# Pooled projection computed channel-major, its running sums by doubling on VectorE and GpSimd in place of banded products on TensorE, and three waits moved

## What is computed

```python
def multiscale_pool(xp):                      # windows 2, 4, 8, 16 for four groups of 256 channels
    cs = pad(cumsum(xp, axis=1))
    lo = maximum(t + 1 - w, 0); cnt = minimum(t + 1, w)
    means[g] = (cs[t + 1] - cs[lo]) / cnt     # mean over the last w tokens
    return concatenate(means) - xp
mix = multiscale_pool(xp)
yb = einsum('bsgc,gcd->bsgd', mix, pool_w) * pool_scale * silu(zp)
```

## Time and profile before

| | |
|---|---|
| median of three runs | 789.54 us |
| the profiled execution's own time | 788.85 us |
| its span (first to last instruction) | 787.0 us |
| PE busy | 775.4 us, 99% |
| DVE busy | 558.2 us, 71% |
| ACT busy | 440.7 us, 56% |
| POOL busy | 131.9 us, 17% |
| granted PE clock | full speed in every slice but the start |

### The profile page before, as it was taken

The page is one execution under the profiler, slowest core; times in us unless marked ns, Lnnn a source line. Parts: engine busy times, 40 slices in busy tenths (PEclk is TensorE's granted clock), DMA queues, the critical chain, the costliest instruction groups (busy, mean ns, idle before and its releaser), DMA issues.

```text
span 787.0 us, 11898 instructions
## 1 busy us (share of the span) xinstructions
PE 775.4 (99%) x4592; PEld 682.2 (87%) x4592; DVE 558.2 (71%) x899; ACT 440.7 (56%) x613; POOL 131.9 (17%) x103
## 2 busy tenths in 40 slices
PE   9999999999999999999999999999999999999998
PEld 7777778888888899999988888999799878978886
DVE  5655565885468687787873476688875896898785
ACT  6755674345443575565644374555856344889650
POOL 0002930000000004444441000014005000006000
PEclk9999999999999999999999999999999999999999
DMA  9987434344454565554545446435465416544211
GB/s 339 406 292 250 177 137 157 134 138 157 170 203 161 199 235 199 183 193 167 207 162 202 177 148 222 151 118 201 161 239 189 156 59 214 202 173 161 107 55 54
DMA packets 23364, 142.78 MB, mean 181 GB/s; under 512 B 3564, under 2 KB 4472, under 8 KB 7312
## 3 DMA queue, kind: packets, MB, share of 16 engines
q1 hardware_dynamic: 20160, 134.51, 47.7%
q10 hardware_dynamic: 1776, 4.12, 1.4%
q0 software_dynamic: 1376, 3.43, 1.2%
HBM read 140.97 MB, written 2.64 MB: 182 GB/s over the span
## 4 chain that ended last, share of the span: by engine, by line
PE 83%; DVE 8%; DMA 3%; ACT 3%; issue 2%; SPq 0%; ACTq 0%; DVEq 0%
PE gemm L496 16%; PE gemm L498 16%; PE gemm L497 16%; PE gemm L502 8%; PE gemm L504 8%; PE gemm L503 8%; DMA raw<-in_weights 2%; DVE wlo L1744 2%; DVE xc L2290 2%; ACT whi L1201 2%; PE head L560 1%; DMA xres<-in_x 1%; PE head L779 1%; PE head L935 1%; PE head L913 1%
## 5 line engine op out<-in xcount | busy, mean ns | idle before, releaser
L1744 DVE TENSOR_TENSOR wlo<-raw,whi 128x2048 fp32r<-128x2048 f32 x119 | 275.6, 2317 | 102.7 <-ACT whi L1201 102.6
L1201 ACT CAST whi<-raw 128x2048 fp32r<-128x2048 f32 x120 | 228.8, 1907 | 193.3 <-PE gemm L498 114.9
L496 PE MATMUL gemm<-whi,x0hi 128*128 128x512 f32 (+2 forms) x400 | 157.7, 394 | 1.0 <-DVE wlo L1744 1.0
L498 PE MATMUL gemm<-whi,x0lo 128*128 128x512 f32 (+2 forms) x400 | 154.0, 385 | 0.0
L497 PE MATMUL gemm<-wlo,x0hi 128*128 128x512 f32 (+2 forms) x400 | 153.6, 384 | 0.0
L502 PE MATMUL gemm<-x1hi,whi 128*128 128x256 f32 x400 | 113.6, 284 | 0.0
L504 PE MATMUL gemm<-x1hi,wlo 128*128 128x256 f32 x400 | 113.2, 283 | 0.0
L503 PE MATMUL gemm<-x1lo,whi 128*128 128x256 f32 x400 | 113.2, 283 | 0.0
L496 PEld LDWEIGHTS gemm<-whi,x0hi 128*128 128x128 f32 x400 | 75.1, 188 | 17.5 <-DVE wlo L1744 2.3
L498 PEld LDWEIGHTS gemm<-whi,x0lo 128*128 128x128 f32 x400 | 75.1, 188 | 15.0
L497 PEld LDWEIGHTS gemm<-wlo,x0hi 128*128 128x128 f32 x400 | 75.2, 188 | 13.4
(11 more groups left out here) (367 smaller groups left out, 1328.3 us busy)
## 6 DMA issues: line engine op xcount, KB each, us to landing
raw<-in_weights SPq DMA_DIRECT2D x122, 1024.0 KB, 4.8
raw<-in_weights SPq DMA_DIRECT2D x4, 512.0 KB, 6.2
bias_rows<-bias_row POOLq DMA_DIRECT2D x1, 1536.0 KB, 19.6
memt<-in_memt SPq DMA_DIRECT2D x4, 256.0 KB, 5.2
tok<-in_mem SPq DMA_DIRECT2D x1, 1024.0 KB, 7.1
xt<-in_xt SPq DMA_DIRECT2D x2, 512.0 KB, 10.9
xres<-in_x ACTq DMA_DIRECT2D x1, 1024.0 KB, 9.1
bias<-bias_rows POOLq DMA_DIRECT2D x8, 128.0 KB, 5.2
```

The costliest lines, as they stand in the source:

```text
L496: mm(o, xh, wh, start=start, stop=False)
L498: return mm(o, xl, wh, start=False, stop=stop)
L1201: nc.scalar.copy(whi[:, p % RING, :], raw[:, p % RING, :]).then_inc(s_hi, 1)
L1744: V.tensor_tensor(wlo[:, p % RING, :], raw[:, p % RING, :], whi[:, p % RING, :].bitcast(F32), ALU.subtract).then_inc(s_lo, 1)
```

## The change

- `xp` becomes channel-major (`crossed_channels`), 48 matmuls a piece. DVE scales it by `rrow` while it empties it into `xpc`, which has 8 zero columns ahead of each channel's 256 tokens. `row_copy(2)` moves from step 78 to the end of step 77 on ACT.
- `pool_mix` goes. Sums over 2, 4, 8 and 16 tokens are made by doubling: a tile plus itself shifted by 1, 2, 4, 8 columns. DVE does groups 0 and 1 at step 78 and group 2 at step 79, POOL group 3. DVE then corrects the first 16 tokens, divides and subtracts `xp` in place (`window_mean`), for all four groups.
- `x1hi` and `x1lo` are made from `xpc` in SBUF, not from PSUM, one step earlier (79 to 82).
- ACT splits piece 85 early in step 83; DVE does so after it has emptied the `pool` chunks, no longer before.
- At step 82 DVE empties `zp` and makes `x1lo` before the gate rows.
- `dm` has its own place, so POOL no longer waits for `s_mixm` ahead of its DMAs; the 1 MB constant `poolb` becomes the small `icnt`.
- The three waits: squares of `mix` at step 4; the first `down` (and `aout`) piece does its two column halves in turn and waits for each half's bank alone; the split of piece 123 comes ahead of the last `olo`.

```diff
-    ("xp", 4, 2, "act"), ...
+    ("xp", 4, 2, "dve"), ...
-SCALED = {"mem": 0, "mix": 3, ...
+SCALED = {"mem": 0, "mix": 4, ...
-LATE_SPLIT = (p0("pool"), p0("up"), ...
+LATE_SPLIT = (p0("up"), ...
...
+            def crossed_channels(p, name, i_):
+                c = c0(name) + i_ % 2
+                if i_ < 2:
+                    chunk_free(pe, c - 2)
+                r = p % RING
+                for b in range(4):
+                    for j in range(4):
+                        kb = 4 * (i_ // 2) + j
+                        ws = slice(j * 512 + b * P, j * 512 + b * P + P)
+                        i = passes_t(bank(c, b // 2)[:, b % 2 * S:b % 2 * S + S], x0hi[:, kb, :], x0lo[:, kb, :],
+                                     whi[:, r, ws], wlo[:, r, ws], kb == 0 and b % 2 == 0, kb == KB - 1 and b % 2 == 1)
+                return i
...
-            def pool_mix(p):
...
                 elif name in ("down", "aout"):
-                    if i_ == 0:
-                        chunk_free(pe, c - 2)
-                        chunk_free(pe, c - 1)
-                    for t in range(T):
-                        for h in range(2):
+                    for h in range(2):
+                        if i_ == 0:
+                            chunk_free(pe, c - 2 + h)
+                        for t in range(T):
                             i = k_major(p, name, i_, h, t, src, i_ == 0, False)
...
+                if p == p0("xp") + 2:
+                    row_copy(2)
+                if p0("zp") <= p < p0("pool"):
+                    b = p - p0("zp")
                     act.wait_ge(s_mixm, b + 1)
+                    nc.scalar.copy(x1hi[:, 2 * b:2 * b + 2, :], xpc[:, 2 * b:2 * b + 2, PAD:PAD + S]).then_inc(s_mixhi, 1)
...
+            def window_sums(g):
+                chunk_free(dve, c0("xp") + g // 2)
+                if g:
+                    dve.wait_ge(s_mixm, g)
+                x = xpc[:, 2 * g:2 * g + 2, :]
+                for k in range(g + 1):
+                    d = 1 << k
+                    order(V.tensor_tensor(wsum[:, k % 2, :, PAD:PAD + S], x[:, :, PAD:PAD + S],
+                                          x[:, :, PAD - d:PAD - d + S], ALU.add))
+                    x = wsum[:, k % 2, :, :]
+                window_mean(g, x)
+            def window_mean(g, x):
+                order(V.tensor_tensor(x[:, :, PAD:PAD + POOL_W], x[:, :, PAD:PAD + POOL_W],
+                                      icnt[:, g, :].unsqueeze(1).broadcast_to([P, 2, POOL_W]), ALU.mult))
+                xg = xpc[:, 2 * g:2 * g + 2, PAD:PAD + S]
+                V.scalar_tensor_tensor(xg, x[:, :, PAD:PAD + S], 1.0 / (2 << g), xg, ALU.mult,
+                                       ALU.subtract).then_inc(s_mixm, 1)
+            def pool_dve(p):
+                if p == p0("zp") + 2:
+                    dve.wait_ge(s_wsum, 1)
+                    window_mean(3, wsum_p[:, 1, :, :])
+                if p0("zp") <= p < p0("pool"):
+                    b = p - p0("zp")
+                    dve.wait_ge(s_mixhi, b + 1)
+                    V.tensor_tensor(x1lo[:, 2 * b:2 * b + 2, :], xpc[:, 2 * b:2 * b + 2, PAD:PAD + S],
+                                    x1hi[:, 2 * b:2 * b + 2, :].bitcast(F32), ALU.subtract).then_inc(s_mixlo, 1)
...
+                    if e == MLA_H + 3:
+                        split(piece_of(e + 1))
...
+                    elif name == "xp":
+                        if n == 0:
+                            V.memset(xpc[:, :, 0:PAD], 0.0)
+                            order(V.memset(wsum[:, :, :, 0:PAD].rearrange("p a b s -> p (a b) s"), 0.0))
+                            dve.wait_ge(s_rrow, 2)
+                        for t in range(T):
+                            k = 4 * n + 2 * t
+                            i = V.tensor_tensor(xpc[:, k:k + 2, PAD:PAD + S],
+                                                bank(c, t)[:, :].rearrange("p (b s) -> p b s", b=2),
+                                                rrow[:, :].unsqueeze(1).broadcast_to([P, 2, S]), ALU.mult)
...
+                if p == p0("zp") + 3:
+                    empty(p)
+                    pool_dve(p)
                 gates_dve(p)
+                if p != p0("zp") + 3:
+                    pool_dve(p)
+                if p in (p0("xp") + 3, p0("zp")):
+                    pool_sums(p)
...
-                if p == p0("pool"):
-                    split(p + 2)
...
-                empty(p)
+                if p != p0("zp") + 3:
+                    empty(p)
+                if p == p0("pool"):
+                    split(p + 2)
...
+            chunk_free(pool, c0("xp") + 1)
+            x = xpc[:, 6:8, :]
+            for k in range(4):
+                d = 1 << k
+                i = Q.tensor_tensor(wsum_p[:, k % 2, :, PAD:PAD + S], x[:, :, PAD:PAD + S],
+                                    x[:, :, PAD - d:PAD - d + S], ALU.add)
+                x = wsum_p[:, k % 2, :, :]
+            i.then_inc(s_wsum, 1)
...
-            pool.wait_ge(s_mixm, 4)
```

More of the change, by code:

```diff
@@ L30 @@
 POOL_W = 16
+PAD = POOL_W // 2
 PHASES = [
@@ L109 @@
 CQ_STEP = p0("ukv") + 1
-SCALED = {"mem": 0, "mix": 3, "ckv": p0("cu") + 3, "cq": p0("ukv")}
+SCALED = {"mem": 0, "mix": 4, "ckv": p0("cu") + 3, "cq": p0("ukv")}
 RS = {"mem": 1, "mix": 2, "ml": 3, "mla": 4, "ckv": 5, "cq": 6}
@@ L144 @@
 REL_STEP = 4
-LATE_SPLIT = (p0("pool"), p0("up"), p0("xp") - 1, p0("xp"), p0("xp") + 1, p0("cu") - 1, p0("cu"), p0("cu") + 1)
+LATE_SPLIT = (p0("up"), p0("xp") - 1, p0("xp"), p0("xp") + 1, p0("cu") - 1, p0("cu"), p0("cu") + 1)
 PARTED = p0("cu") + 3
@@ L194, in program @@
         [[tok], [hthi, htlo, gbuf, ubuf, gfin],
-         [ybhi, yblo, om, xmhi, xmlo, zm, xc], [_1, _2, _3, q_ml, k_ml], [_4, _5, _6, xp, zp],
+         [ybhi, yblo, om, xmhi, xmlo, zm, xc], [_1, _2, _3, q_ml, k_ml],
+         [_4, _5, _6, wsum_p, _20, zp, xpc, wsum],
          [cz, qn_c, qp_c, kn_c, v_c, kpe, cu, cqhi, cqlo], [_7, _8, _9, _10, _11, _12, ohi, olo]] = overlay(
@@ L218, in program @@
         prob_t = sb("prob_t", [P, 2, 512])
-        [[bias, decay, rcos, rsin, onehot, brows], [poolb, mtri, mmla, invf, _13, rows, csin, ccos, ang, kpr]] = overlay(
+        [[bias, decay, rcos, rsin, onehot, brows], [dm, icnt, _21, mtri, mmla, invf, _13, rows, csin, ccos, ang, kpr]] = overlay(
             8192 + RET_H * TRI * 4 + 1024 + 3 * TRI * 4,
@@ L330, in program @@
         s_rc = sem("rotary_loaded")
-        s_zero = sem("zeros_ready")
+        s_zero, s_wsum = sem("zeros_ready"), sem("window_sums_ready")
         s_hm = sem("ml_h_gated")
@@ L1587, in empty @@
                                              ACT.Tanh, scale=0.5).then_inc(s_tanh, 1)
-                    elif name == "xp":
+                    elif name == "om":
                         if n == 0:
                             act.wait_ge(s_rs, RS["ml"])
[L1591 to L1595, removed]
                             act.wait_ge(s_yblo, 4)
@@ L2277, in mla_tail @@
                         z_gate((e - 2) // 4)
-                    if e % 2:
+                    if e % 2 and e != MLA_H + 3:
                         split(piece_of(e + 1))
@@ L2364, in _ @@
                     split_half(3, 1)
-                elif p not in LATE_SPLIT and p > 0:
+                elif p not in LATE_SPLIT and p > 0 and p != p0("pool"):
                     split(p + 2)
@@ L2394, in _ @@
                     turn_lo(name, which)
[L2395 to L2403, removed]
                 if p == p0("ukv"):
@@ L2543, in constants @@
     to_tiles = lambda a: a.reshape(T, P, -1).transpose(1, 0, 2).reshape(P, -1)
[L2544 to L2549, removed]
+    first = np.arange(1, POOL_W + 1)
+    icnt = np.concatenate([w / np.minimum(first, w) for w in (2, 4, 8, 16)])
     mtri = np.where(q[None, :] < i[:, None], NEG, 0.0)
```

40 lines of the change are left out of this document (23 added, 17 removed).

## The result

The changed kernel takes 783.5 us at the median (783.11 to 784.0, six runs), the kernel before beside it 789.67 (788.83 to 790.79, six runs). The ratio is 0.9922, 95% interval 0.9909 to 0.9935: 6.2 us faster, where 3.2 were forecast. The profiled execution has a span of 782.2 us and an own time of 784.0, the slowest of its six.

The account below looks back on a forecast made before the run. It took PE as the bound, with DVE equally so in the tap steps; 1.0 us from the pool stage and 2.2 from three waits made 3.2, so 786.3 us (by itself 785 to 788; whole range 782.6 to 789.6).

Parts of the forecast that it names:

- first rival: PE stays the bound: DVE absorbs its new work and the pool stage gains the whole 4.3 us; 783.0 us, chance 0.22.
- PE's net saving, 3.8 us: Pool steps on PE: banded products removed, 5.1 us, less 1.3 us for four longer `xp` pieces.
- DVE's added work, 10.2 us: Pool steps on DVE: scalings, adds, subtractions, corrections and memsets; 8.0 us net once the split of piece 85 leaves.
- What POOL does to DVE: Pool steps: POOL's four adds of 1.3 us hold DVE for 0 to 5.2 us; the upper end, 5.2, was taken.
- PE's wait of some 3 us: Pool stage: PE's 0.46 us wait for DVE grows to some 3 us, part of it at `zp`'s third piece.
- the sign: In the profile after, a PE wait of 1 us or more at `zp`'s third piece or at piece 83 or 84.
- The stage's gain is kept: After the pool stage: the tap steps follow DVE, which starts the `pool` chunks 1.0 us earlier, so 1.0 us is kept.
- half order of `aout`: At `aout`: doing the column halves in turn changes nothing, as ACT has emptied both chunks by then.
- The three waits, 2.2 us: Squares of `mix` 0.8 us, first `down` piece 1.0, last split 0.4: together 2.2 us gained.
- The second rival: DVE eats more than PE gives: the pool stage loses 1.5 us, waits give 2.2; 788.8 us, no change, chance 0.17.
- The third: Rival: POOL's adds are slow in themselves, 3.2 us each, deciding from 2.1 us an add; 793.9 us, slower, chance 0.11.

Follow-up runs that it names:

- e7: The changed kernel with the squares of `mix` taken back to step 3: 784.49 us.
- e2: The changed kernel with the three moved waits put back as they were before: 787.09 us.
- e8: The changed kernel with ACT's copy of the bias rows ahead of the split of piece 6 instead of behind it: 783.46 us.
- e9: e4 with POOL's mask additions held back until DVE has done the first group's four tap steps, and ACT's two decay steps moved later: 781.52 us.
- e3: The changed kernel without POOL's four window additions, group 3's mean taken from group 2's sums, so its output is wrong: 783.52 us.
- e5: The changed kernel with POOL's four window additions done twice, with the same values: 786.14 us.
- e4: The changed kernel with group 3's four additions on DVE, behind the split of piece 83, and none on POOL: 782.12 us.
- e6: The changed kernel with DVE's split of piece 85 ahead of emptying the `pool` chunks again, as before: 786.66 us.
- e10: e5 with ten extra PE products on a constant ahead of piece 81, where PE stood idle: 786.39 us.

## Why the prediction was right, and where it was not

The direction and the chain were right, the size was half. 783.5 is below the 785 to 788 that the forecast gave itself; only the wider range, drawn down to the first rival's end, holds it. 786.3 was forecast and 783.5 measured: 2.8 us, of which 2.0 are the stage's (2.96 for 1.0) and the rest, 0.8, the waits' (some 3.0 for 2.2).

- *PE's net saving, 3.8 us.* By the start-to-start times over the whole stretch, the banded products took 5.13 us (5.1 forecast) and the four `xp` pieces became 1.2 longer (1.3). What I left out stands behind each group: the second matmul of the next piece starts 0.20 us behind the first where 0.12 is usual, 0.3 in all. Net 4.2.
- *DVE's added work, 10.2 us.* Every row came out as taken from its like: scalings 1.29 a pair, additions 0.69 of length and 0.73 from start to start, corrections 0.19. The memsets took 0.2. Less the moved split, and with POOL's holds, the windows show 11.0 us more work; 8.0 + 2.8 is 10.8.
- *What POOL does to DVE, 5.2 us.* This is the step that failed: the term "What POOL does to DVE", which measured 2.8. I took the least length of a POOL addition in the trace, 1.3 us, as its length alone; it is 1.04. And I took the upper end because DVE's chain leaves gaps. But the chain holds POOL off as well (2.04 an addition in the mean), and part of the work fell into a wait of DVE for ACT. The 2.4 us are DVE's lateness that I forecast and that did not come.
- *PE's wait of some 3 us.* It is 0.73 + 0.72, where 0.46 was. The first stands in the last part of piece 83, one of the places named; neither reaches the 1 us that I gave as the sign. Counted from start to start, the two cost 1.2 us more than the one of before: 4.2 - 1.2 = 3.0, the stage's gain.
- *The stage's gain is kept.* Right in the main: from piece 84 to `cu` within 0.1 us in the changed kernel's trace and in e7's. In those of e2 and e8, whose program is the same there, the masks start 8.8 and 8.7 us behind the issue of their DMA, not 7.0 and 7.1, meet `xmlo` and the taps, and PE loses 0.5 us. So how much is kept hangs on when the masks land. The split of piece 85 now meets POOL's `yblo` (11.22 us, before 7.11), and two splits of DVE take 6.21 us for some 4.5; PE waits for neither. The new half order of `aout` and the dropped load moved nothing, as said. The mask additions still held DVE in the tap steps, for about as long as before; with all sums on DVE e9 shows that they cost 0.95 us between piece 84 and `wv`, and 0.6 of the median.
- *The three waits, 2.2 us.* All three mechanisms were right, and nothing came behind them. The term was mis-sized: 1.0, 1.2 and 0.7 for 0.8, 1.0 and 0.4. For `down` and the tail I took the wait as the profile labels it. That idle time is counted from the modelled end of the last matmul, 0.28 us behind its start with the next one due 0.12 behind it (0.39 and 0.23 for the longer form), so a wait costs 0.16 us more than its label. The rest stands behind the wait: the second matmul starts 0.34 us behind the first where 0.23 is usual (0.31 at `down`), and the next few a hundredth late each. That makes 0.1 to 0.2 us a wait, which I had left out for the squares too, though I had counted those from start to start.
- *The rivals.* The median lies next to the first rival's 783.0, but it was not that mechanism: its mark was that PE waits for DVE nowhere between pieces 79 and 91, and it waits twice. Its 4.3 us for the stage appears only in e3, without POOL's additions. The second rival would need a stage that loses; e5 is what it looks like, with twice the POOL work: 0.12 gained. The third needs 2.1 us an addition for DVE; an addition takes POOL 2.04 in the mean, but DVE is not idle beside it and loses 0.7 for each.

## What to carry to other kernels

When two engines hold each other off, take the length of each one's instruction alone and count what falls into waits that are there anyway; the lengths in a trace of the contended stretch contain the other's work. And an engine that stands idle is not in itself a reason to share the work out: here DVE did POOL's four additions itself (e4) and came out 1.4 us ahead, since its own idle time and the holds together were longer than the work.

Read a wait's cost from start to start, not from its label. When an experiment removes work from one engine, read the stage and not only the total: e3 gained 1.4 us in the stage and, in its trace, gave it to a collision 20 us later.

## What was not expected of the hardware

The clock fell behind two waits of PE that the experiments made: 2.0 us in e5 (503 us, mean clock 0.57 over the next four us) and 2.9 us in e6 (522 us, 0.66 over 4.4 us); each cost PE about 1.5 us on top of the wait. The cause was tested in e5's case alone. Behind the waits of 0.7 to 1.3 us in this stage, in any of the kernels, it stayed at 1.00. So the price of the split's place in e6 was half as much again as the split: 2.2 of work and 1.5 of clock, less the 0.35 that came back. Whether the clock's loss reaches the time is another matter, as e10 shows.

A channel-major piece of 48 matmuls over 256 columns takes 5.75 us, and a token-major one of 24 over 512 columns 5.44: twice the instructions for the same columns cost 6%.
